# Two query tiles, or two key branches, in one softmax unit of the first block's attention, and another order of its jobs

## What is computed

```python
xn = rms_norm(x, norm1_g)
aq, ak, av, bq, kc, vc, ksl, vsl, kw, vw, gl = split_columns(xn @ w_in)
o_a = mixer_dilated(aq, ak, av, table_a)              # 8 heads: softmax(q k / 8 + bias) v
kcmp, vcmp = nsa_compress(kc, ...), nsa_compress(vc, ...)   # 15 compressed tokens per group, by an MLP
# 8 heads in 2 groups share K and V; three branches, each weighted by its gate:
o_b = g0 * compressed(q, kcmp, vcmp) + g1 * selected(q, ksl, vsl) + g2 * window(q, kw, vw)
h = x + concat(o_a, o_b) @ w_out
```

## Time and profile before

| | |
|---|---|
| median of 3 runs | 3179.72 us (3179.25 to 3185.11) |
| the profiled execution's own time | 3177.99 us |
| its span | 3176.2 us |
| PE busy | 2966.4 us, 93% of the span |
| DVE, ACT, POOL busy | 865.9, 717.2, 236.9 us |
| first product of the first block | 18.10 us |
| first product of w_out | 235.76 us |

### The profile page before, as it was taken

How to read it: one execution, slowest core, us unless ns; L and a number is a source line. 1 busy time by engine, 2 the same in 40 slices (tenths; PEclk the granted TensorE clock), 3 DMA queues, 4 the chain that set the end, 5 groups by cost and what they waited for, 6 DMA issues and landing times. The chain is left out here.

```text
span 3176.2 us, 31060 instructions
## 1 busy us (share of the span) xinstructions
PE 2966.4 (93%) x12390; PEld 1877.5 (59%) x12390; DVE 865.9 (27%) x1597; ACT 717.2 (23%) x1697; POOL 236.9 (7%) x259
## 2 busy tenths in 40 slices
PE   7989998799999799899998999997999899998998
PEld 6757887355555566544443444443666577787887
DVE  1231101455454433310112110004555623201100
ACT  1230000255554433200001000001444422201100
POOL 3000000023232100000000000000222200000000
PEclk9869999899999899899999999998999999999999
DMA  9205867233333111122222453432443322254552
GB/s 220 71 21 152 249 188 216 58 102 101 81 101 92 35 52 53 47 73 73 80 73 82 144 148 97 126 96 67 121 106 100 87 60 67 73 153 126 150 149 73
DMA packets 529871, 330.42 MB, mean 104 GB/s; under 512 B 27472, under 2 KB 496832, under 8 KB 529728
## 3 DMA queue, kind: packets, MB, share of 16 engines
q1 hardware_dynamic: 518896, 296.36, 33.0%
q0 software_dynamic: 10256, 30.41, 4.0%
q10 hardware_dynamic: 576, 1.66, 0.1%
HBM read 327.05 MB, written 1.34 MB: 103 GB/s over the span
## 5 line engine op out<-in xcount | busy, mean ns | idle before, releaser
L911 PE MATMUL ps<-xnT,W 128*128 128x512 f32 (+2 forms) x4064 | 1346.2, 491 | 62.2 <-ACTq L387 44.3
L911 PEld LDWEIGHTS ps<-xnT,W 128*128 128x128 f32 (+1 forms) x4064 | 780.7, 194 | 593.0 <-issue 470.6
L911 PE MATMUL ps<-BIG,W 128*128 128x256 f32 (+1 forms) x2528 | 773.6, 468 | 11.5 <-ACTq L387 9.0
L911 PEld LDWEIGHTS ps<-BIG,W 128*128 128x128 f32 x2528 | 481.3, 191 | 301.8 <-issue 247.3
L1710 DVE SCALAR_TENSOR_TENSOR TMP<-ps,prmT,TMP 128x510 f32<-128x510 f32 (+3 forms) x256 | 182.5, 714 | 141.1 <-ACT TMP L708 126.3
L546 ACT ACTIVATE xnT<-hT 128x256 f32<-128x256 f32 (+1 forms) x56 | 23.0, 493 | 631.0 <-DVEq L387 631.0
L495 POOL DMA_DIRECT2D cs_rows<-BIG x2 | 1.1, 564 | 1753.8 <-DVE BIG L1752 1753.8
L1630 DVE SCALAR_TENSOR_TENSOR hT<-ps,modc,hT 128x256 f32<-128x256 f32 x48 | 21.8, 481 | 398.1 <-PE ps L911 398.1
L1318 PE MATMUL ps<-W,xnT 128*128 128x128 f32 x1024 | 122.6, 276 | 0.0
L521 POOL TENSOR_TENSOR BIG<-BIG,TMP 128x512 f32<-128x512 f32 x80 | 108.3, 1367 | 188.5 <-ACT BIG L741 188.4
L1318 PEld LDWEIGHTS ps<-W,xnT 128*128 128x128 f32 x1024 | 118.3, 192 | 3.4 <-issue 3.3
(11 more groups left out here) (244 smaller groups left out, 2248.3 us busy)
## 6 DMA issues: line engine op xcount, KB each, us to landing
W<-in_w_in SPq DMA_DIRECT2D x192, 512.0 KB, 4.0
W<-in_w_mlp SPq DMA_DIRECT2D x128, 512.0 KB, 4.0
W<-in_ada_w SPq DMA_DIRECT2D x96, 512.0 KB, 4.6
BIG<-cs_rows POOLq DMA_DIRECT2D x96, 256.0 KB, 4.7
W<-in_w_ssd_o SPq DMA_DIRECT2D x32, 512.0 KB, 4.0
W<-in_w_gate SPq DMA_DIRECT2D x22, 512.0 KB, 7.9
W<-in_w_up SPq DMA_DIRECT2D x22, 512.0 KB, 6.3
W<-in_w_down SPq DMA_DIRECT2D x16, 512.0 KB, 4.1
```

The source lines that it names most:

```text
L911: last = mm(dst, w[:, c, 0:m], rhs(k), start=k == 0, stop=k == total - 1)
```

## The change

Order and pieces (13 steps in place of 26; job A3 comes after B3, with A3q, A3k, A3v in steps 8 to 10, among the units of B2 and B3):

```diff
-JOBS = ["A0", "B0", "A1", "B1", "A2", "B2", "A3", "B3"]
-STEPS = [("A0", 1), ("A0", 0), ("C", 0), ("C", 1)]
+JOBS = ["A0", "B0", "A1", "B1", "A2", "B2", "B3", "A3"]
+STEPS = [("A0",), ("C",)]
 for _j in JOBS[1:]:
-    STEPS += ([(_j, 1), (_j, 0)] if _j[0] == "A" else
-              [(_j, 1, "sel"), (_j, 1, "win"), (_j, 0, "sel"), (_j, 0, "win")])
+    STEPS += [(_j,)] if _j[0] == "A" else [(_j, 1), (_j, 0)]
...
-FILL = {0: (("c0",), ("c1",)), 1: (("B01a", "B01b"), ("B23a", "B23b", "mlp", "Bka", "Bkb", "cmp")),
-        2: (("Bva",), ("Bvb",)), 3: (("Bg",), ("A1q",)), 4: ((), ("A1k",)), 5: ((), ("A1v",)),
-        6: (("h0",), ("h1",)), 7: (("h2",), ("h3",)), 8: ((), ("A2q",)), 9: ((), ("A2k",)), 10: ((), ("A2v",)),
-        11: (("h4",), ("h5",)), 12: (("h6",), ("h7",)), 13: (("par1",), ("par2",)), 14: ((), ("A3q",)),
-        15: ((), ("A3k",)), 16: ((), ("A3v",)), 17: ((), ("par3",)), 18: ((), ("par4",)), 19: ((), ("par5",))}
+FILL = {0: (("c0", "c1"), ("B01a", "B01b", "B23a", "B23b", "mlp", "Bka", "Bkb", "cmp")), 1: (("Bva",), ("Bvb", "Bg")),
+        2: (("A1q",), ("A1k",)), 3: (("A1v",), ("h0",)), 4: (("A2q",), ()), 5: (("A2k",), ()), 6: (("A2v",), ("h1",)),
+        7: (("h2", "h3"), ("par1",)), 8: (("A3q",), ()), 9: (("A3k",), ()), 10: (("A3v",), ()),
+        11: (("h4", "h5"), ("par2",)), 12: (("h6", "h7"), ("par3", "par4", "par5"))}
```

An A unit now holds both query tiles, a B unit both branches of one query tile, C all of it. Four blocks of scores per unit stand in banks 2 and 3, one bank per head; the same two banks serve every step:

```diff
+        def blocks(u):
+
+            if u[0][0] == "A":
+                return [(h, at, qt, P * (qt + 1)) for qt, at in ((1, 0), (0, S)) for h in range(2)]
+            nk = P * (u[1] + 1)
+            return [(h, br * nk, u[1], nk) for h in range(2) for br in range(2)]
...
-            def scores(s, h):
+            def scores(s):
                 u = STEPS[s]
-                b = PS[2 + s % 3]
-                if h:
-                    pe.wait_ge(s_s0, s + 1)
-                elif s >= 3:
-                    pe.wait_ge(s_mx, s - 2)
+                if s:
+                    pe.wait_ge(s_mx, s)
...
+                    todo = blocks(u)
+                    if u[0][0] == "B":
+                        todo = [todo[0], todo[2], todo[1], todo[3]]
+                    for h, at, qt, nk in todo:
+                        q = qkA[:, i % 2, 0, :] if u[0][0] == "A" else qB[:, i, :]
+                        k = qkA[:, i % 2, 1, :] if u[0][0] == "A" else kB[:, int(at > 0), :]
+                        last = mm(PS[2 + h][:, at:at + nk], q[64 * h:64 * h + 64, qt * P:(qt + 1) * P],
+                                  k[64 * h:64 * h + 64, 0:nk], start=True, stop=True)
+                last.then_inc(s_sc, 1)
```

C's 32 small score matmuls go in one group too, with the two row halves in turn. `turn` writes all of a unit's transpositions (A 6, B 8 or 4, C 4) to banks 4 and 5, `turned` copies them in one instruction (768, 1024 or 512 columns, C 512), `values` does all products of a unit in one group. PE's pipeline is one step shorter:

```diff
-            for s in range(len(STEPS) + 3):
+            for s in range(len(STEPS) + 2):
                 if s < len(STEPS):
-                    scores(s, 0)
+                    scores(s)
                 fill(s, 0)
-                if s >= 3:
-                    values(s - 3)
-                if s < len(STEPS):
-                    scores(s, 1)
-                if 2 <= s < len(STEPS) + 2:
-                    turn(s - 2)
+                if s >= 2:
+                    values(s - 2)
+                if 1 <= s <= len(STEPS):
+                    turn(s - 1)
                 fill(s, 1)
```

At the start:

```diff
             pool.dma_start(biasraw, bass.AP(tensor=line_dram, offset=0, ap=[[1, P], [LINE, 16], [1, S]]))\
                 .then_inc(bias_in, 16)
+            pool.dma_start(xin[:, 2:4, :], a["ctx_2"][0].rearrange("(t p) d -> p t d", p=P)).then_inc(in_ctx, 16)
...
-            act.dma_start(xin[:, 2:4, :], a["ctx_2"][0].rearrange("(t p) d -> p t d", p=P)).then_inc(in_ctx, 16)
...
...
-            act.wait_ge(g1_t, 1)
-            copy(prmT[:, 0, 0:8], PS[6][:, 0:8]).then_inc(g1_e, 1)
             for t in range(2):
                 act.wait_ge(x_ms[t], 1)
                 A(small[:, 50 + t:51 + t], small[:, 50 + t:51 + t], ACT.Sqrt).then_inc(x_rt[t], 1)
+            act.wait_ge(g1_t, 1)
+            copy(prmT[:, 0, 0:8], PS[6][:, 0:8]).then_inc(g1_e, 1)
```

More of the change, by code:

```diff
@@ L628, in turned @@
                 if u[0] == "C":
-                    last = copy(PTc[:, :, u[1], :], PS[5][:, 0:S].rearrange("p (g q) -> p g q", g=2))
+                    last = copy(PTc.rearrange("p g q n -> p (g q n)"), PS[4])
                 else:
@@ L632, in turned @@
                         act.wait_ge(s_pv, values_until(s - 2))
-                    n = 2 * P * (u[1] + 1)
-                    last = copy(PT[:, s % 2, 0:n], PS[5][:, 0:n])
+                    n = P * sum(nk // P for _, _, _, nk in blocks(u))
+                    last = copy(PT[:, s % 2, 0:n], PSA[:, 4:6, :].rearrange("p b n -> p (b n)")[:, 0:n])
                 last.then_inc(s_pt, 1)
@@ L639, in _ @@
                     keep(x)
-            for s in range(len(STEPS) + 2):
+            for s in range(len(STEPS) + 1):
                 if s < len(STEPS):
@@ L1105, in values @@
-                opens = len(u) == 2 or u[2] == "sel"
-                closes = len(u) == 2 or u[2] == "win"
-                for n, term in enumerate(terms):
-                    for h, (lhs, rhs) in enumerate(term):
-                        last = mm(out[64 * h:64 * h + 64, qt * P:(qt + 1) * P], lhs, rhs,
-                                  start=opens and n == 0, stop=closes and n == len(terms) - 1)
+                evicted(u[0] + "v" if u[0][0] == "A" else "Bvb")
+                first = {}
+                n = 0
@@ new lines, in values @@
+                for j, (h, at, qt, nk) in enumerate(blocks(u)):
+                    first[j] = n
+                    n += nk // P
+                for qt in ((1, 0) if u[0][0] == "A" else (u[1],)):
+                    terms = []
+                    if u[0][0] == "B":
+                        terms.append([(vcmp[32 * i:32 * i + 32, h, :], PTc[32 * i:32 * i + 32, h, qt, :]) for h in range(2)])
+                    pairs = [(0, 1)] if u[0][0] == "A" and qt else [(2, 3)] if u[0][0] == "A" else [(0, 2), (1, 3)]
+                    for br, pair in enumerate(pairs):
+                        for kb in range(qt + 1):
+                            v = vA[:, i % 2, kb, :] if u[0][0] == "A" else vB[:, br, kb, :]
+                            terms.append([(v[:, 64 * h:64 * h + 64],
+                                           PT[:, s % 2, (first[j] + kb) * P:(first[j] + kb + 1) * P])
+                                          for h, j in enumerate(pair)])
+                    for n, term in enumerate(terms):
+                        for h, (lhs, rhs) in enumerate(term):
+                            last = mm(out[64 * h:64 * h + 64, qt * P:(qt + 1) * P], lhs, rhs,
+                                      start=n == 0, stop=n == len(terms) - 1)
@@ new lines, in maximum @@
+                    for g in range(2):
+                        for qt in range(2):
+                            V.scalar_tensor_tensor(
+                                out=SC[:, s % 3, g, qt * P:(qt + 1) * P].rearrange("p (r n) -> p r n", n=32)[:, :, 0:15],
+                                in0=PS[2 + g][:, qt * P:(qt + 1) * P].rearrange("p (r n) -> p r n", n=32)[:, :, 0:15],
+                                scalar=HD ** -0.5, in1=cst[:, C_CMP + 15 * qt:C_CMP + 15 * qt + 15].unsqueeze(1)
+                                .to_broadcast([P, 4, 15]), op0=ALU.mult, op1=ALU.add)
@@ L1536, in maximum @@
                         .then_inc(s_mx, 1)
[L1537 to L1541 removed]
+                    return
@@ new lines, in weighted @@
+                    return
+                V.reciprocal(c[:, 8:12], c[:, 4:8])
+                dve.drain()
+                for j, (h, at, qt, nk) in enumerate(blocks(u)):
+                    p = SC[:, s % 3, h, at:at + nk]
+                    if u[0][0] == "A":
+                        last = V.tensor_scalar(p, p, c[:, 8 + j:9 + j], None, ALU.mult)
+                    else:
+                        gate = gate1[:, qt, span(12 * h + 3 * int(u[0][1]) + 1 + (at > 0), 1)]
+                        last = V.tensor_scalar(p, p, c[:, 8 + j:9 + j], gate, ALU.mult, ALU.mult)
@@ L1574, in job_out @@
+                last.then_inc(s_pn, 1)
             def job_out(s):
@@ L1591, in _ @@
                                 windows(x)
-                if s >= 4 and last_of_job(s - 4):
-                    job_out(s - 4)
+                if s >= 3 and last_of_job(s - 3):
+                    job_out(s - 3)
             dve.wait_ge(in_small, 16 * 13)
```

154 lines of the change are left out of this document (67 added, 87 removed).

## The result

The changed kernel took 3123.03 us (median; 3122.36 to 3126.39) against 3179.48 us before, a ratio of 0.9822 with an interval of 0.9805 to 0.9839. The profiled execution took 3122.36 us with a span of 3120.6.

The account below looks back on a forecast made before the run. PE was taken as the bound, badly used in the head before w_out. Start -1.0 and end of cmp to w_out -39.1 (17.9+89.8+7=114.7 against 153.8) gave 3177.99-40.1+1.7=3140 us; range 3127 to 3162.

Parts of the forecast that it names:

- the start: Before B01a: first product 2.65 us earlier, bias table landing at 40.0, B01a at 43.2, low clock charged 1.7; net -1.0 us.
- mlp to the end of cmp: From B01a to 82.0 us: same instructions, PE covers DVE and ACT, change 0.
- C with Bva, Bvb, Bg: From the end of cmp to B0's scores: C's scores, three products, A0's turn, wait and boundaries, 17.9 us.
- steps 2 to 6 and 8 to 10, with products: Units from B0 on with a product beside them: PE's scores, product, values, turn and boundaries, 64.5 us.
- steps 7 and 11: Units with only h and par pieces, so no product covers DVE's chain: 6.2 and 5.8 us.
- step 12 and tail to job_out's end: Last unit as a pure chain from scores through maximum, exponentials, weighting, turn, copy and values to job_out: 10.6 us.
- job_out to w_out: From job_out to the first product of w_out: 2.65 us, as before.
- the clock: Low stretches after Bg (2.5 us), at step 7 (1.7) and in the tail (3): 7 us in all, ends 0 and 30.
- more: Rival, 10%: no low clock and the table 3 us earlier, -50 us, 3130.
- Scores without overlap: Rival, 15%: scores don't overlap (+6, C +1.5) and low clock holds half the units (+12): about -20, 3160.
- The slower clock: Rival, 6%: PE at 1.2 GHz from C to w_out, +18 us, 3198.
- The bias table: Rival, 4%, no gain: the table's readback lands at 75 us or later and DVE holds B01a that long.

Follow-up runs that it names:

- a3_early: The changed kernel with job A3 ahead of B3 again: 3124.4 us, ratio to before 0.9829.
- the square: Four kernels compared: 3179.5 us with neither half, 3140.7 with the doubling of units alone, 3139.4 with the heads' score overlap alone, 3123.0 with both.
- overlap_before: The kernel before, only with both heads' scores issued together into separate banks without the wait between them: 3139.4 us, ratio to before 0.9874.
- half_units: The changed kernel with small units again (25 steps), keeping its start, job order, score overlap and short pipeline: 3162.4 us, ratio to before 0.9951.
- deep_double: The changed kernel with the pipeline as deep as before (turn of s-2, values of s-3): 3125.9 us, ratio to before 0.9832.

## Why the prediction was wrong in size

**What held.** The sign, the place (all of it before w_out), the start and everything behind w_out. The start was -1.0 forecast and -0.8 measured at mlp: first product 15.48 (15.45), the table's landing releasing DVE at 40.15 (40.0), B01a at 42.95 (43.2), a low stretch behind the stand. mlp to the end of cmp was unchanged, 20.7 us in both. DVE's and ACT's new shapes came within 5%. That the start came out so close is partly luck: the low stretch cost 2.6 us and not 1.7, while B01a came 0.25 us early and a score group that had stood among the products (53.30 in the kernel before, 0.4 us) was gone; and a3_early shows what one start can differ by.

**The steps that failed.** From the end of cmp (81.1) to w_out I had 114.7 us, the trace has 99.4. By terms:

| term | forecast | measured |
|---|---|---|
| C with Bva, Bvb, Bg (81.1 to 95.85) | 17.9 | 14.75 |
| steps 2 to 6 and 8 to 10, with products | 64.5 | 58.7 (1.6 of it low clock) |
| steps 7 and 11 | 12.0 | 11.5 |
| step 12 and tail to job_out's end (178.27) | 10.6 | 12.3 (1.1 of it low clock) |
| job_out to w_out | 2.65 | 2.2 |
| the clock | 7 | in the rows above, 2.7 |

First, the groups were priced too high: "Product 3.9 with its boundary" was taken with another 0.4 to 0.5 us of boundaries per step, which the 3.9 already held, and scores and values carried 0.2 us each that starts in the timeline don't show (scores of B 1.06 for 1.3, values 0.95 for 1.1). Eight steps by 0.9 us, 7.4 in all: step 5, forecast 7.7, is 6.8. "Head 1's first pass can run beside head 0's second" was too cautious. From start to start the scores took 0.85 (A), 1.06 (B, tile 1) and 0.65 (B, tile 0) where I took 1.05, 1.3 and 0.75; the other sum that I weighed, half of the stream, had 0.85, 1.05 and 0.6. That the gaps of 0.26 us agree with a drain isn't borne out: the same gap stands between two full-array products (52.93 above), and none stands ahead of the scores at 120.34, where the tiling changes too. Second, "The clock. ... 7 in all": it cost 2.7, and C was priced with products at the durations that they had in part at the low clock; 82 to 96 us ran at 1.00. Against these the tail was 1.7 us longer than its chain: 1.1 is the low clock, and for the rest PE stood in the par pieces and values of step 11 when the last weighting was ready at 172.3, and turned only at 174.10.

These are terms of one mechanism that was right, but the account of it was not. I had split the 40 us into scores, groups and waits, with the clock as a small charge against the gain. The runs show that the terms don't add up: 38 to 40 us came with either half alone, in the builds of the square, and most of the low clock went with it. The range's lower end, 3127, came from the same dear groups; even "more", with no low clock and the table 3 us earlier, only reached 3130. 3123 lay below it.

**The rivals.** Scores without overlap: false (1.13 us, half of 2.31). The slower clock: false; over the units it rose from 0.73 to 0.94. The bias table: it does gate B01a, but with 6.9 us of PE's stand and not 40. "More" named no low clock and an earlier table; the low clock nearly went, the table did not come earlier.

**Open.** How many us of the 56 the clock alone is worth, up to some 29, and in overlap_before how much is the overlap, how much is one score group per step in place of two, and how much the clock. Whether the two halves need separate banks. What the order is worth with doubled units. half_units differs from overlap_before in depth, start and order together.

## What to carry to other kernels

Matmuls of two 64-row halves belong side by side without a semaphore between them (here in different PSUM banks): it halved them, and in the kernel with small units and the deep pipeline it was worth as much as doubling the units, with the time at 1.2 GHz down from 69 to 18 us. Two such edits are not priced by adding what each gives alone. And before a load is moved ahead or behind, look at whose packets hold the engines: beside POOL's large ones a tile of SP's 256-byte pieces took 28.1 us to land, and holding them back until the first products are done moved mlp from 60.4 to 52.9 us, of which 4 to 5 us are left in the total.

## What the runs showed of the hardware that was not expected

A high busy share of PE does not mean a full clock: PE was busy 17.1 of 18 us in 155 to 173 of the kernel before, at a mean clock of 0.53, and 21.8 of 24 in 131 to 155 of the change, at 1.00. The low level itself makes the instructions longer, so the share doesn't give the cause. The rows of before show what PE did: the clock was full up to about 155, where PE had stood 1.57 us for ACT among small groups, and rose behind the product at 168.13:

```profile
154.49 0.82 PE L1024 MATMUL ps<-cst,BIG 128*128 128x128 f32 x4 [1.57 <-ACT hT L540]
...
168.13 5.49 PE L911 MATMUL ps<-xnT,W 128*128 128x256 f32 x16
```

And 16 us of added full-array work cost nothing in the total that could be measured (ratio 0.9994). Where a low stretch falls can differ between executions of the same code: C's scores and the product behind them ran at full clock in the change and partly at the low one in deep_double, which is the same up to there.
